# A mixer and 16 experts on one core: other block order, weight chunks fetched in pairs

## What is computed

```python
def expert_block(args):
    xb, e = args
    a, b = jnp.split(xb @ w_gu[e], 2, axis=-1)
    return (jax.nn.silu(a) * b) @ w_dn[e]
```

## Time and profile before

| | |
|---|---|
| device time, 3 runs | 877.03 us median (876.08 to 877.6) |
| the profiled execution | 879.71 us |
| its span | 877.9 us |
| TensorE busy | 850.3 us (97%) |
| PEld / DVE / ACT / POOL busy | 493.2 / 407.1 / 256.3 / 59.4 us |
| mean granted TensorE clock | 0.986 |
| moved by DMA | 258.06 MB, mean 294 GB/s |

### The profile page before, as it was taken

One profiled execution on the slowest core, in us unless ns is written; L12 is line 12 of the kernel. 1 busy time (PEld: TensorE's weight loads), 2 busy tenths in 40 slices (PEclk: granted clock), 3 DMA queues, 4 the chain that ended last, 5 costly groups with the idle time before them and its releaser, 6 DMA issues.

```text
span 877.9 us, 16475 instructions
## 1 busy us (share of the span) xinstructions
PE 850.3 (97%) x7102; PEld 493.2 (56%) x7102; DVE 407.1 (46%) x666; ACT 256.3 (29%) x465; POOL 59.4 (7%) x75
## 2 busy tenths in 40 slices
PE   9999999999999999999898899999999999999996
PEld 7889798777888888633232453556533333333332
DVE  5588877686687575782221133121021212212247
ACT  6223535354358232431222011211122210211212
POOL 2200000000000000101010100000010000000203
PEclk9999999999999999999898999999999999999998
DMA  9822131313223369999999999999999999999992
GB/s 347 341 97 97 57 136 49 144 49 120 96 56 136 101 239 408 422 351 358 409 377 395 398 416 416 414 398 408 377 419 376 420 400 409 417 407 411 422 367 101
DMA packets 43704, 258.06 MB, mean 294 GB/s; under 512 B 5466, under 2 KB 5614, under 8 KB 18416
## 3 DMA queue, kind: packets, MB, share of 16 engines
q1 hardware_dynamic: 37584, 239.16, 68.8%
q0 software_dynamic: 6048, 17.86, 5.4%
HBM read 245.93 MB, written 13.42 MB: 295 GB/s over the span
## 4 chain that ended last, share of the span: by engine, by line
PE 88%; DMA 7%; ACT 2%; DVE 1%; issue 1%; SPq 0%; POOL 0%; POOLq 0%; DVEq 0%
PE ps L1102 21%; PE ps L740 12%; PE ps L741 11%; PE ps L745 11%; PE ps L1125 10%; PE ps L1113 7%; PE ps L1148 4%; DMA raw_e<-in_expert_w_gate_up 3%; PE ps L1137 2%; PE ps L787 2%; DMA xe<-x1n,slots 1%; PE ps L1162 1%; DMA x1n<-x 1%; PE ps L1085 1%; DMA xe<-x1n,gidx 1%
## 5 line engine op out<-in xcount | busy, mean ns | idle before, releaser
L1102 PE MATMUL ps<-raw_e,xt_strip 128*32 128x512 f32 x1888 | 206.0, 592 | 0.1
L1102 PEld LDWEIGHTS ps<-raw_e,xt_strip 128*32 128x32 f32 x1888 | 60.7, 110 | 138.1 <-issue 135.7
L2118 DVE TENSOR_TENSOR strip<-strip,ps 64x1536 f32<-64x1536 f32 (+2 forms) x18 | 24.2, 1343 | 202.7 <-ACT strip L1548 202.7
L740 PE MATMUL ps<-xh,hi_m 128*128 128x512 f32 x272 | 108.0, 397 | 0.0
L741 PE MATMUL ps<-xl,hi_m 128*128 128x512 f32 x272 | 106.2, 390 | 0.0
L1548 ACT ACTIVATE strip<-ps 64x1536 f32<-64x1536 f32 (+2 forms) x18 | 20.0, 1110 | 257.5 <-PE ps L1102 188.1
L1125 PE MATMUL ps<-raw_e,hT 128*32 128x512 f32 x752 | 87.1, 603 | 2.6 <-DMA raw_e<-in_expert_w_down 2.6
L1679 DVE SCALAR_TENSOR_TENSOR cacc<-hg,cwt,cacc 128x512 f32<-128x512 f32 x120 | 82.0, 744 | 0.0
L1647 DVE TENSOR_TENSOR lo_m<-raw_m,hi_m 128x2048 fp32r<-128x2048 f32 x27 | 61.8, 2290 | 41.4 <-ACT hi_m L1369 41.3
L1113 PE MATMUL ps<-raw_e,xt_strip 128*32 128x256 f32 x1280 | 71.5, 385 | 1.6 <-DMA raw_e<-in_expert_w_gate_up 1.6
L745 PE MATMUL ps<-xh,lo_m 128*128 128x512 f32 x272 | 67.2, 389 | 0.0
(11 more groups left out here) (328 smaller groups left out, 936.7 us busy)
## 6 DMA issues: line engine op xcount, KB each, us to landing
raw_e<-in_expert_w_gate_up SPq DMA_DIRECT2D x126, 1024.0 KB, 20.5
raw_e<-in_expert_w_down SPq DMA_DIRECT2D x60, 1024.0 KB, 20.6
raw_m<-in_w_in_chunks SPq DMA_DIRECT2D x20, 1024.0 KB, 5.0
yd<-zeros POOLq DMA_DIRECT2D x8, 512.0 KB, 7.0
raw_m<-in_w_o SPq DMA_DIRECT2D x4, 1024.0 KB, 5.1
yt<-yd SPq DMA_DIRECT2D x4, 1024.0 KB, 13.3
raw_m<-in_w_conv_out SPq DMA_DIRECT2D x2, 1024.0 KB, 5.7
x<-in_x POOLq DMA_DIRECT2D x1, 2048.0 KB, 16.8
```

The lines of the kernel that those rows point to most:

```text
L740: pe.matmul(dst, a1, b1, start=first, stop=False)
L1102: mm = pe.matmul(ps[at_, bank + g], xt[:, c, g * STRIP:(g + 1) * STRIP], cols[s], start=(c == 0), stop=(c == GU - 1))
```

## The change

1. The blocks' strips become 2, 3, 1, 2, 1, 6, 1, 4, 1, 3, 3, 3, 3, 3, 2, 2. `WIDE` (6 strips) is block 5 and `HALVED` (4) block 7.
2. The ring becomes 8 places of 16 KB a partition. Two chunks that follow each other are fetched by one transfer of 2 MB whose runs are 16 KB on both sides, into both halves of a place, once both chunks that were there are used; one semaphore says that both have landed. For that the host arranges the weights so that a partition's rows of two chunks lie side by side. Half gate chunks stay two transfers of 1 MB with runs of 4 KB, under one semaphore.
3. Fetches ahead: the kept-apart gate chunk is 6 instead of 5, and half of it and a half of `down_1` go out at mixer chunk 12 in the place of ring place 0; nothing goes out at 23; places 2 and 3 of the pairs wait for the last mixer chunk's cut and for `wo_used` 3; four pairs (8 MB) wait for `wo_done`.
4. The norm rows are fetched behind scatter 0; the final LayerNorm's are spread inside block 4's gate step, gain and shift inside those of blocks 7 and 8. The transposes of the second row tile wait for `lnf_sb` and no longer for `x1_ready`.
5. The wide block's second rows get gain and shift on DVE (`second_rows`), beside ACT.
6. `x1` lies 8 KB further on; `gate_1`, `xe`, `down_1` use the old place 0.

```diff
-EARLY = (5, 7, 26, 27, 28, 29)
+EARLY = (6, 7, 26, 27, 28, 29)
 GU, DN = 8, 4
 TAB = 32
 MAXOV = TAB - 1 - NE
@@ -61,10 +61,10 @@
 PIECES = ((0, 1), (1, 2), (2, 3), (3, 4), (4, 6), (6, 8))
 
 
-SHARE = (2, 3, 1, 1, 1, 4, 2, 6, 1, 3, 3, 3, 3, 3, 2, 2)
-WIDE = 7
+SHARE = (2, 3, 1, 2, 1, 6, 1, 4, 1, 3, 3, 3, 3, 3, 2, 2)
+WIDE, HALVED = 5, 7
 ROUTER_OPS = 15
-BY_PLACE = (0, 1, WIDE, 5, 9, 10, 11, 12, 13, 6, 14, 15, 2, 3, 4, 8)
+BY_PLACE = (0, 1, WIDE, HALVED, 9, 10, 11, 12, 13, 3, 14, 15, 2, 4, 6, 8)
...
-        RAW_KB = (184.5, 160, 168.5, 176.5, 152, 40, 48, 32, 0, 16, 56, 72, 64, 80, 8, 24)
-        raw_e = [at(f"raw_e{s}", [P, CH], F32, RAW_KB[s]) for s in range(RE)]
+        PAIR_KB = (168.5, 152, 32, 48, 64, 80, 0, 16)
+        RAW_KB = [kb + 8 * c for kb in PAIR_KB for c in range(2)]
+        raw_p = [at(f"raw_p{m}", [P, 2 * CH], F32, PAIR_KB[m]) for m in range(RE // 2)]
+        raw_e = [raw_p[s // 2][:, s % 2 * CH:(s % 2 + 1) * CH] for s in range(RE)]
...
-        gate_1 = [at(f"gate_1{k}", [P, D], F32, (104, 124)[k]) for k in range(2)]
-        xe = [at(f"xe{s}", [P, D], F32, (104, 213.8125)[s]) for s in range(2)]
+        gate_1 = [at(f"gate_1{k}", [P, D], F32, (184.5, 124)[k]) for k in range(2)]
+        xe = [at(f"xe{s}", [P, D], F32, (184.5, 213.8125)[s]) for s in range(2)]
         down_0 = at("down_0", [P, CH], F32, 205.8125)
-        down_1 = [at(f"down_1{k}", [P, D], F32, (108, 217.8125)[k]) for k in range(2)]
+        down_1 = [at(f"down_1{k}", [P, D], F32, (188.5, 217.8125)[k]) for k in range(2)]
...
-        SHARED = {5: 1, 6: 2, 7: 0}
-        raw_in = [raw_in_m[SHARED[s]] if s in SHARED else sem(f"raw_in{s}") for s in range(RE)]
-        M_USES = [len(range(SHARED[s] or RM, NM, RM)) if s in SHARED else 0 for s in range(RE)]
+        raw_in = [sem(f"raw_in{m}") for m in range(RE // 2)]
...
-        wgu_v = expert_w_gate_up.rearrange("a e (k p) c -> (a e) k p c", p=P)
-        wgh_v = expert_w_gate_up.rearrange("a e (j k p) (h c) -> (a e) h j p k c", p=P, k=2, h=2)
-        wdn_v = expert_w_down.rearrange("a e (c p k) n -> (a e) c p (k n)", p=P, k=2)
+        wgu_v = expert_w_gate_up.rearrange("a e (m p d) n -> (a e) m d p n", p=P, d=2)
+        wgp_v = expert_w_gate_up.rearrange("a e (m p d) n -> (a e) m p (d n)", p=P, d=2)
+        wgh_v = expert_w_gate_up.rearrange("a e (m d p k) (h n) -> (a e) h m p d k n", p=P, d=2, k=2, h=2)
+        wdn_v = expert_w_down.rearrange("a e (m p d k) n -> (a e) m d p (k n)", p=P, d=2, k=2)
+        wdp_v = expert_w_down.rearrange("a e (m p d) n -> (a e) m p (d n)", p=P, d=4)
...
+        def transfers(slot, before):
+
+            return sum(1 + (q in SPLIT) for q in range(before) if ring_slot(q) == slot)
+
         def landed(p):
 
-            s = ring_slot(p)
-            return 16 * (M_USES[s] + sum(ring_slot(q) == s for q in range(p + 1)))
+            return 16 * transfers(ring_slot(p), p + 1)
...
+            def fetch(slot, src, half=None):
+
+                assert slot % 2 == 0
+                dst = raw_p[slot // 2]
+                if half is None:
+                    sp.dma_start(dst, src).then_inc(raw_in[slot // 2], 16)
+                    return
+                dst = dst.rearrange("p (d k n) -> p d k n", d=2, k=2)
+                for d in range(2):
+                    sp.dma_start(dst[:, d], src[:, d]).then_inc(raw_in[slot // 2], 16)
...
+            def load(p, src, half=None):
+
+                sp.wait_ge(chunk_used, freed_by(p + 1) + 1)
+                fetch(ring_slot(p), src, half)
 
             def load_late(p, slot, src):
 
-                sp.wait_ge(chunk_used, p - 11)
+                sp.wait_ge(chunk_used, p - 10)
...
+                    gate_early(0)
+                    sp.dma_start(down_1[0], wdn_v[1, 0, 1][:, 0:D]).then_inc(down_in[1], 16)
+                if n == 16:
+                    sp.dma_start(down_0, wdn_v[1, 0, 0]).then_inc(down_in[0], 16)
+                if n == 18:
+                    sp.dma_start(down_1[1], wdn_v[1, 0, 1][:, D:]).then_inc(down_in[1], 16)
+                if n == NM - 1:
+                    sp.wait_ge(proj_done, 50)
                     fetch_ring(0)
-                if n == 16:
-                    sp.dma_start(down_0, wdn_v[1, 0]).then_inc(down_in[0], 16)
-                if n == 18:
-                    sp.dma_start(down_1[1], wdn_v[1, 1, :, D:]).then_inc(down_in[1], 16)
-                if n == 23:
-                    sp.wait_ge(cb_T, CT)
-                    fetch_ring(1)
-                elif n == NM - 1:
-                    sp.wait_ge(proj_done, 50)
-                    fetch_ring(2)
-                    fetch_ring(3)
                 sp.dma_start(in_tiles(raw_m[n % RM], n), mixer_source(n)).then_inc(raw_in_m[n % RM], 16)
 
             sp.wait_ge(m_ready, KT)
...
             sp.wait_ge(m_ready, KT)
-            fetch_ring(4)
-            sp.dma_start(gate_0, early[EARLY[1]]).then_inc(gate_in[1], 16)
+            fetch_ring(1)
+            sp.dma_start(gate_0, wgu_v[0, EARLY[1] // 2, EARLY[1] % 2]).then_inc(gate_in[1], 16)
             sp.wait_ge(proj_done, 58)
+            gate_early(1)
+            sp.dma_start(raw_0, wdn_v[0, 1, 0]).then_inc(ahead_in, 16)
             for k in range(2):
-                sp.dma_start(gate_1[k], early[EARLY[0]][:, k * D:(k + 1) * D]).then_inc(gate_in[0], 16)
-            sp.dma_start(down_1[0], wdn_v[1, 1, :, 0:D]).then_inc(down_in[1], 16)
-            sp.dma_start(raw_0, wdn_v[0, DN - LATER]).then_inc(ahead_in, 16)
-            for k in range(2):
-                sp.dma_start(raw_1[k], wdn_v[0, DN - 1, :, k * D:(k + 1) * D]).then_inc(ahead_in, 16)
-            for slot in (5, 6, 7):
-                sp.wait_ge(lo_ready, NM - 7 + slot)
-                fetch_ring(slot)
-            sp.wait_ge(wo_used, 2)
-            for slot in (8, 9):
-                fetch_ring(slot)
+                sp.dma_start(raw_1[k], wdn_v[0, 1, 1][:, k * D:(k + 1) * D]).then_inc(ahead_in, 16)
+            sp.wait_ge(lo_ready, NM)
+            fetch_ring(2)
             sp.wait_ge(wo_used, 3)
-            for slot in (10, 11):
-                fetch_ring(slot)
+            fetch_ring(3)
             sp.wait_ge(wo_done, NT + 1)
-            for slot in range(12, RE):
-                fetch_ring(slot)
+            for m in range(4, RE // 2):
+                fetch_ring(m)
...
-                elif i == 1:
+                elif i == 0:
...
-                    pe.wait_ge(x1_ready, NT)
+                    pe.wait_ge(lnf_sb, 1)
...
+            def spread_last():
+
+                pe.wait_ge(ln_in, 64)
+                pe.wait_ge(ye_ready, 2)
+                spread(2, (2, 4))
+                spread(3, (1, 5))
+
+            def spread_gain():
+
+                pe.wait_ge(ye_ready, WIDE + 1)
+                spread(0, (2, 5))
+
+            def spread_shift():
+
+                pe.wait_ge(ln1_gain, NT)
+                spread(1, (2, 5))
+
+            SPREADS = {(WIDE - 1, None): {3: spread_last}, (HALVED, 0): {2: spread_gain},
+                       (HALVED + 1, None): {1: spread_shift}}
...
+            def second_rows():
+
+                dve.wait_ge(xe_T, WIDE)
+                dst = rows_of(WIDE)
+                for k in range(KT):
+                    ins = dve.tensor_scalar(dst[:, k, P:P + HALF], ps[:, 5, k * HALF:(k + 1) * HALF],
+                                            gb[:, 0, k:k + 1], gb[:, 1, k:k + 1], ALU.mult, ALU.add)
+                ins.then_inc(xt_ready, 1)
...
-    arranged = {"expert_w_gate_up": gate_up.reshape(1, NE, D, 2 * FF)}
+    gate_up = gate_up.reshape(NE, GU // 2, 2, P, 2 * FF).transpose(0, 1, 3, 2, 4)
+    down = np.asarray(inputs["expert_w_down"]).reshape(NE, DN // 2, 2, P, 2, D).transpose(0, 1, 3, 2, 4, 5)
+    arranged = {"expert_w_gate_up": gate_up.reshape(1, NE, D, 2 * FF), "expert_w_down": down.reshape(1, NE, FF, D)}
```

More of the change, by code:

```diff
@@ L93, in freed_by, with rows_at @@
     return max(q for q in range(p) if ring_slot(q) == ring_slot(p))
+def rows_at(i):
+    return i + (not isinstance(i, int) or i >= WIDE)
 def banks_of(j):
@@ L521, in load_late, with fetch_ring @@
+            def load(p, src, half=None):
+                sp.wait_ge(chunk_used, freed_by(p + 1) + 1)
+                fetch(ring_slot(p), src, half)
             def load_late(p, slot, src):
[L523 removed]
+                sp.wait_ge(chunk_used, p - 10)
                 fetch(slot, src)
[L526 to L531 removed]
+            def fetch_ring(m):
+                p = [q for q in range(RE + AHEAD - LATER) if ring_slot(q) == 2 * m][0]
+                fetch(2 * m, down_source(0, 0) if p >= 2 * GU else gate_source(p // GU, None, p % GU // 2))
@@ L533, in _, with gate_early @@
+            def gate_early(k):
+                c = EARLY[0]
+                sp.dma_start(gate_1[k], wgu_v[0, c // 2, c % 2][:, k * D:(k + 1) * D]).then_inc(gate_in[0], 16)
             for p, (k0, k1) in enumerate(PIECES):
@@ L582, in _ @@
```

(37 more changed lines are left out.)

83 lines of the change are left out of this document (28 added, 55 removed).

## The result

The kernel with the change takes 885.72 us (median of 5 runs, 883.96 to 887.72), the kernel before 877.6 beside it: ratio 1.0094, interval 1.008 to 1.0108. The forecast of 882.5 (869 to 892) had the sign and two thirds of the size (5.5 of 8.2 us). The profiled execution took 886.59 us against 879.71, with a span of 884.9.

The account below looks back on a forecast made before the run. DMA chains lead at the expert part's start and weight chunks at 504.6 us, then TensorE almost to the end. 879.7 + 5.5 = 885.2 us for the profiled execution; the median is 2.7 below, 882.5 us, range 869 to 892.

Parts of the forecast that it names:

- The other queue: Expert part's start: queues alternate run by run, so x1n's store takes +4.3 us, the gather +1.8; transposes at 394.4.
- The clock: At block 1's start: the 7 us wait lowers TensorE's granted clock, costing 2.8 us; TensorE 9 us late from here.
- Chunk 47: First refills: issued 9 us later, and +2.5 for carrying 2 MB, so it lands 11.5 us late.
- the early loads: Before wo_done: SP's queue empty until 355, about 6 us of DMA time lost, only some of it felt.
- The longer runs: Chunks 47 to 187: 16 KB runs reach 423 GB/s, saving 0.03 us a chunk over 132 chunks, -4.3 us.
- rival 2: Weight fetches: larger transfers truly faster, 435 GB/s, 13 us gained over 132 chunks, time 875 us; chance 0.06.
- The order: From chunk 64: 17.2 us of TensorE on offer; it ends block 8 6 us early, then waits for DMA.
- The end: Last chunks: chunk 187 +6 us, last two land at about 857, TensorE's end 5.5 us later.
- The wait for ACT's second rows: By block 8's end: TensorE no longer waits for these rows, 1.9 us less.
- (1): At 388 us: TensorE not delayed, queues share by bytes or x1n lands before the 8 MB; 872.5 us, chance 0.27.
- (3): Weight fetches: 16 KB runs are cut into 8 KB ones, no delay and no saving; 877.5 us, chance 0.09.
- (4): Small blocks: runs no faster, gathers and stores 2 to 3 us later, clock drops twice more; 890 us, chance 0.12.

Follow-up runs that it names:

- runs8k: Kernel after the change, but each pair fetched by two 1 MB transfers with runs of 8 KB; 881.41 us, ratio 1.0051.
- late_singles: Kernel before with the new block order and ring of single chunks, four early fetches put behind wo_done; 879.06 us, ratio 1.0017.
- early_halves: Kernel after with 8 KB runs up to chunk 23, and halves of places fetched as they come free, in the earlier schedule; 878.13 us, ratio 1.0003.
- short_start: Kernel after, with 8 KB runs for the pairs up to chunk 23 and 16 KB from chunk 24 on; 878.29 us, ratio 1.0003.
- fine_start: Kernel after, but single chunks with 8 KB runs in the earlier early-load schedule up to chunk 55, then pairs with 16 KB runs; 876.66 us, ratio 0.9989.
- order_only: Kernel before with only the new block order, spreads and second rows on DVE, its ring of 16 single chunks kept; 876.13 us, ratio 0.9992.
- last_first: Kernel after, with the last pair issued ahead of the wait for the outputs and the first read-back; 885.74 us, ratio 1.0091.
- pairs_only: Kernel before with only the ring of pairs, early loads and x1's place, the old block order kept; 893.67 us, ratio 1.0181.
- hold_gather: Kernel after, with three of the four pairs at wo_done held back until block 1's rows are gathered; 889.54 us, ratio 1.0134.

## Why the prediction was right

**The other queue** was the step that decided, and its mechanism held; its largest term was too small. Store +4.3 was forecast (4.8 by the plain sum), +6.1 measured; gather +1.8 and +1.4; transposes 394.4 and 395.4; block 1's first gate chunk 9 us late and 9.7 (402.7 for 393.0). Of the 6.1 us, 5.1 are the length of the runs (16.7 for 11.6 in runs8k). The other 1.0 comes with 8 MB queued instead of 4 (11.6 for 10.6), which the forecast did not price. The slope of 0.32 us a run says that the plain 4.8 was the better number; the 0.5 that I took off for overlap shows nowhere. The Trainium skill (DMA: Bandwidth & Descriptors, Queues, rings and completion order) has an engine drain some 9 to 17 descriptors of a ring before it switches; as the prediction works out, the gather would by that have grown by 5 us. It grew by 1.4, so this store and this gather speak for single turns.

**The clock** cost what was said (2.8 us forecast): the transposes, the gate chunk and the 16 records behind it take 1.51, 3.57 and 2.21 us for 0.85, 1.85 and 1.96, which is 2.6 more. With the 7.0 us of waiting that makes the 9.7. But the next stall cost nothing: granted 1.00 from 406 to 505 us where the earlier trace rows have 0.93, and 72 records in 7.93 us for 10.71. Net TensorE was 6.9 us late by chunk 30, not 9. The forecast had no reason for that, and the traces give none (last section).

**Chunk 47** was forecast 11.5 us late and landed at 464.9, 11.2 late. The sum is right, its parts are not, and that they add up is luck. The fetch was issued at 454.9, 6.9 us later and not 9, and it took 10.0 us for 5.7, 4.3 more and not 2.5. runs8k, where TensorE is on time, lands it at 457.1: only 7.8 us come from the long runs and 3.4 from the coarse places and the late loads, where I had 9 and 2.5 and took the early loads for absorbed. This is the step that was sized wrong: "only some of that is felt". late_singles puts 2.2 us on late loads, runs8k another (1.0051 - 1.0017) x 877.5 = 3.0 on the places being pairs. The two kernels differ in a few more fetches, so the division between these two is rough; and by early_halves, where late loads bring nothing back, the places alone would be worth all of it. (Between 366 and 406 us have a share of 0.91; the forecast reads 0.89.)

**The longer runs** give -4.2 us (runs8k to short_start) for the -4.3 forecast, though over 148 chunks and not 132. The stage 720 to 730 us, read as in the earlier trace rows, has 424 GB/s for 418; 423 was forecast. A pair in the quiet stretch of the kernel after takes 4.9 us: the two issued at 719.93 and 726.13 landed 36.1 and 34.8 us later, at 756.0 and 760.9; 2 x 2.51 was the price before. That is 428 GB/s, still below the 435 of rival 2. The Trainium skill (DMA: Bandwidth & Descriptors, Measured) has 425 GB/s for 16 MB and 341 for 1 MB, issued from GpSimd. Queued back to back from SP, the size of a transfer made no such difference here.

That is a gain against the same pairs with shorter runs. Against single chunks none was measured: fine_start has 16 KB runs from chunk 56 on and order_only has none, and their ratios are 0.9989 and 0.9992.

**The order**: by chunk 103, behind block 8's gate, TensorE was 5.1 us ahead (632.6 for 637.7; 6 forecast), and then TensorE met late transfers, from 675 us on. order_only shows that it would have met them without the pairs too.

**The end**: the pair of chunk 187 landed 7.0 us late (6 forecast), the last pair at 857.7 (857), TensorE's last chunk ended 6.9 us late (5.5). What I left out is the scatter of block 14, 11.9 us for 7.9, which holds the last fetch back by 4 us. It depends on the length of the runs as at the start: beside 8 KB runs it takes 6.8 us in runs8k; last_first bounds what that is worth at 1.3 us in the profile and nothing by the medians. The wait for ACT's second rows is gone, but TensorE's transposes of hidden tiles still wait 1.8 us where they waited 2.7: 0.9 us, not 1.9:

```profile
L1164 PE MATMUL ps<-ident,strip 64*128 64x64 f32 x152 | 13.0, 228 | 1.8 <-ACT xt_strip L1571 1.0 <-DVE strip L2129 0.8
```

The profiled execution was forecast at 885.2 and took 886.59, 1.4 us more, which is TensorE's last chunk (6.9 for 5.5). The other 1.8 of the 3.2 us between 882.5 and 885.72 are no part of the mechanism: the median lies 0.9 us below the profiled execution, where I took the 2.7 of the kernel before.

So the 8.2 us are, by ratios: order -0.7, late loads +2.2, coarse places +3.0, 16 KB runs up to chunk 23 +8.0, 16 KB runs behind it -4.2. By the intervals the first two are uncertain by some 1 us, the +8.0 by 1.5, and the two that rest on runs8k by 2. The terms also depend on the order in which they are taken: the new order of blocks is worth 0.7 us alone and 7.6 us once the pairs are there.

**Rivals.** (1) fell with its condition: the delay was 7.0 us. But it was also wrong where the condition holds: with TensorE on time and long runs kept from chunk 24 on (short_start) the time is 878.3, not 872.5, since coarse places and late loads stay. (2) is too high a rate. (3) fell: the trace has the weights as packets of 16 KB, 0.61 us each, and the store grew beside them. (4) saw the gathers rightly (+3.1 us each) and their effect wrongly: behind block 1 TensorE waits for none of them in the kernel after. The range's lower end, 869, does not follow from rival 1, whose own numbers end at 877.0 - 6 = 871.

## What to carry to other kernels

Where two queues share the DMA engines, price a longer run by what the other queue pays: at least one of your runs for each of its own. Long runs were dear where a small dependent chain (store, then gather, then the first matmul) runs through the other queue (8.0 us). Where it carried nothing urgent they gave 4.2 us against the same pairs with 8 KB runs, but nothing was measured against single chunks, whose places come free one by one. Length of run can be chosen by stage; count what the coarser places cost before taking it. When transfers set the end, count the us in which the engines stood idle, and ask of each saving whether it removes some or only moves them.

## What was not expected of the hardware

Two idle stretches of TensorE of the same length had different prices. Both are at the same place of the program, ahead of down chunk 28: 3.4 us before 434.0 in the kernel before, 3.35 us before 443.7 in the kernel after. The 6 us behind each, before and then after:

```profile
434.00:440.00 6.00, 5.98 (x32) 1.74 (x36) 0.65 (x1) 0.02 (x1) 1.87 (x2) 0.53 1.02 423
```

```profile
443.00:449.00 6.00, 5.30 (x52) 2.07 (x56) 1.28 (x2) 0.90 (x4) 4.00 (x6) 1.00 1.00 425
```

The granted clock is 0.53 in the one, half speed (1.2 GHz) for nearly all of it, and 1.00 in the other, full speed (2.4 GHz). TensorE had worked from 388.4 on before the one, at 1.00, and from 395.4 on before the other, with 0.57 granted over 395 to 402 us. The same stall, 3.3 to 3.4 us, stands in all fourteen traces. Twelve of them take 9.4 to 10.7 us for the 72 records behind it; only the kernel after and last_first take 7.93. It isn't the lateness: pairs_only transposes block 1's rows as late as these two, and takes 9.63. What decides wasn't tried, so the 2.8 us that the kernel after got back here are luck.

One turn per run held for the store over three lengths, also with 8 MB queued. But the series doesn't reach down to nothing. Even 4 KB runs made the store 9.4 us for 5.0 in hold_gather, 4.4 us more, where one turn of 0.16 us for each of 16 runs is 2.6. For the gather it is 7.7 for 4.4, 3.3 us more, where 6 runs make 1.0. What the rest is, no run here shows.

For the later row transfers the runs ahead in the same queue have to be counted too. The scatters, mostly of 96 rows, 6 runs an engine, grew by 1.7 us (9.6 for 7.9), 0.28 us a run. The gathers grew by 3.1 us; each is issued some 1.2 us behind a scatter, and over the 12 runs of both that is 0.26 us a run. But the scatter of block 14, 64 rows, grew from 6.8 us in runs8k to 11.9. With the gather of 64 rows issued 2 us before it that is 8 runs an engine and 0.6 us a run, twice the price. Why, wasn't tried.
